# Sample tokens' retention attention cut into four pieces that stand between the weight matmuls of input units 23 and 24

## What is computed

```python
h = rmsnorm(x, g_pre_mix)
p = h @ w_in                     # 3328 columns: a_u a_v | b_b b_c b_x | c_q c_k c_v c_g
a_out = chunk_mlp(a_u, a_v)      # causal mixing in chunks of 128 tokens, 4 heads
b_out = b_b * conv3(b_c * b_x)   # depthwise, width 3, with a carried buffer
c_out = retention(rope(q), rope(k), v) normed per head * silu(c_g)     # 8 heads of 64
x = x + rmsnorm(concat(a_out, b_out, c_out) @ w_out)
x = x + rmsnorm((silu(h2 @ w_gate) * (h2 @ w_up)) @ w_down)            # h2 = rmsnorm(x)
```

```python
o = (q @ k.T * decay_mask) @ v + (q * q_decay) @ S      # S: that sequence's own 64 x 64 state
S = decay * S + (k * k_decay).T @ v
```

## Time and profile before

| | |
|---|---|
| three runs | 1314.28, 1316.05, 1316.15 us; median 1316.05 |
| the profiled execution | 1315.72 us |
| its span, first to last instruction | 1314.0 us |
| mean granted TensorE clock | 0.986 of full speed |
| PE busy | 1283.9 us (98% of the span) |
| DVE busy | 871.9 us (66%) |
| ACT busy | 558.3 us (42%) |
| DMA | 119.1 MB, mean 91 GB/s |

### The profile page before, as it was taken

How to read it: one execution, slowest core, us unless ns; L and a number is a source line. 1 busy time by engine, 2 the same in 40 slices (tenths; PEclk the granted TensorE clock), 3 DMA queues, 4 the chain that set the end, 5 groups by cost and what they waited for, 6 DMA issues and landing times.

```text
span 1314.0 us, 26201 instructions
## 1 busy us (share of the span) xinstructions
PE 1283.9 (98%) x10425; PEld 1253.8 (95%) x10425; DVE 871.9 (66%) x1231; ACT 558.3 (42%) x899; POOL 36.3 (3%) x60
## 2 busy tenths in 40 slices
PE   6999999989999999999999999998999999999997
PEld 6999998989999999999999999898999999999996
DVE  6855778288888787522586566855978787882225
ACT  4632224354355556522443512245444555562222
POOL 3000002000000000000020000010000000000000
PEclk9999998989999999999999999899999999999998
DMA  6322122123333333223242221132223333312321
GB/s 230 97 76 81 56 64 97 53 67 112 112 97 96 96 96 96 73 89 113 80 154 67 84 77 56 63 103 75 75 88 112 98 110 96 96 56 89 113 65 69
DMA packets 110410, 119.10 MB, mean 91 GB/s; under 512 B 4512, under 2 KB 107064, under 8 KB 110072
## 3 DMA queue, kind: packets, MB, share of 16 engines
q1 hardware_dynamic: 107392, 108.57, 26.2%
q0 software_dynamic: 2496, 8.24, 1.8%
q10 hardware_dynamic: 440, 1.09, 0.2%
HBM read 113.20 MB, written 4.69 MB: 90 GB/s over the span
## 4 chain that ended last, share of the span: by engine, by line
PE 90%; DVE 6%; ACT 1%; issue 1%; DMA 1%; ACTq 0%; DVEq 0%; SPq 0%
PE ps L608 20%; PE ps L610 19%; PE ps L609 19%; PE ps L990 8%; PE ps L992 8%; PE ps L991 8%; PE ps L638 1%; PE ps L758 1%; DVE w_lo L1384 1%; PE ps L777 1%; DVE x L1420 1%; PE ps L798 1%; DVE h_lo L1441 1%; DVE r_pre L1457 1%; PE ps L838 1%
## 5 line engine op out<-in xcount | busy, mean ns | idle before, releaser
L608 PE MATMUL ps<-h_hi,w_hi 128*128 128x272 f32 x1216 | 363.7, 299 | 8.9 <-issue 3.7
L610 PE MATMUL ps<-h_lo,w_hi 128*128 128x272 f32 x1216 | 354.1, 291 | 0.0
L609 PE MATMUL ps<-h_hi,w_lo 128*128 128x272 f32 x1216 | 352.7, 290 | 0.0
L1384 DVE TENSOR_TENSOR w_lo<-w_raw,w_hi 128x1024 fp32r<-128x1024 f32 (+1 forms) x140 | 165.1, 1190 | 176.5 <-ACT w_hi L1053 175.9
L990 PE MATMUL ps<-a_hi,p_hi 128*128 128x272 f32 x896 | 260.0, 290 | 2.3 <-DVE evac L1842 2.0
L992 PE MATMUL ps<-a_lo,p_hi 128*128 128x272 f32 x896 | 259.3, 289 | 0.0
L991 PE MATMUL ps<-a_hi,p_lo 128*128 128x272 f32 x896 | 257.9, 288 | 0.0
L608 PEld LDWEIGHTS ps<-h_hi,w_hi 128*128 128x128 f32 x1216 | 232.7, 191 | 17.9 <-issue 10.8
L609 PEld LDWEIGHTS ps<-h_hi,w_lo 128*128 128x128 f32 x1216 | 233.7, 192 | 2.3 <-issue 2.0
L610 PEld LDWEIGHTS ps<-h_lo,w_hi 128*128 128x128 f32 x1216 | 232.0, 191 | 0.0
L1053 ACT ACTIVATE w_hi<-w_raw 128x1024 fp32r<-128x1024 f32 (+1 forms) x140 | 143.2, 1031 | 168.1 <-DMA w_raw<-in_w_down 116.2
(11 more groups left out here) (203 smaller groups left out, 1654.9 us busy)
## 6 DMA issues: line engine op xcount, KB each, us to landing
w_raw<-in_w_in SPq DMA_DIRECT2D x52, 512.0 KB, 3.6
w_raw<-in_w_gate SPq DMA_DIRECT2D x44, 512.0 KB, 3.5
w_raw<-in_w_up SPq DMA_DIRECT2D x44, 512.0 KB, 3.5
w_raw<-in_w_down SPq DMA_DIRECT2D x40, 512.0 KB, 3.3
w_raw<-in_w_out SPq DMA_DIRECT2D x16, 512.0 KB, 3.4
tab<-in_table POOLq DMA_DIRECT2D x2, 1520.0 KB, 6.3
st_s<-in_state_ret POOLq DMA_DIRECT2D x8, 256.0 KB, 4.1
out<-st_s POOLq DMA_DIRECT2D x16, 128.0 KB, 2.2
```

What stands on the lines that cost most here:

```text
L608: pe.matmul(out, wh, hi[:, cols(half)], start=begins, stop=False)
L609: pe.matmul(out, wl, hi[:, cols(half)], start=False, stop=False)
L610: mm = pe.matmul(out, wh, lo[:, cols(half)], start=False, stop=ends)
L1384: vec.tensor_tensor(w_lo[s][:, 0:nk, :], w_raw[s][:, 0:nk, :], w_hi[s][:, 0:nk, :], ALU.subtract)\
```

## The change

`attend_s` is no longer one step behind unit 23. It becomes four pieces: the values matmuls with the state matmuls of head pair 0 stand in the middle of unit 23's second half; the state matmuls of head pair 1 directly behind unit 23, ahead of `norm_o3`; those of head pair 2 in the middle of unit 24's first half; those of head pair 3 and the two transposes in the middle of its second half. The middle of a half is behind two of its four k-tiles, 12 of 24 weight matmuls. The step now counts up `mix_pe` inside unit 24, behind `norm_o3`. Nothing is changed on DVE, ACT, POOL or SP but the counts they wait for.

```diff
-    23: ["attend_s", "norm_o3"], 24: ["norm_o4", "state_s0"], 25: ["state_s1"],
+    23: ["norm_o3"], "within 24": ["attend_s"], 24: ["norm_o4", "state_s0"], 25: ["state_s1"],
...
-            def unit(layer, pos, more, ks, source, group, first, last, done=None, before_half=lambda half: None):
+            def unit(layer, pos, more, ks, source, group, first, last, done=None, before_half=lambda half: None,
+                     mid_half=lambda half: None):
                 for half in range(2):
                     before_half(half)
-                    unit_half(layer, pos, more, ks, source, group, half, first, last, done)
+                    unit_half(layer, pos, more, ks, source, group, half, first, last, done,
+                              after_two=lambda half=half: mid_half(half))
...
-                def attend_s():
+                def attend_s_values():
                     after(probs_made, 5)
                     after(o_made, 4)
...
-                    for hp in range(HP):
-                        for b in range(DB):
...
+                def attend_s_state(hp):
+                    for b in range(DB):
+                        at = NS * hp + DS * b
+                        for e in range(2):
+                            rows = slice(HD * e, HD * e + HD)
+                            pe.matmul(ps[rows, 6, at:at + DS], st_s[rows, hp, b, :], qds[rows, hp, b, :],
+                                      start=False, stop=(b == DB - 1), skip_group_check=True)
+
+                def attend_s_end():
                     after(z_last_made, 1)
                     after(probs_made, 5)
                     for ct in range(2):
                         tr = transpose(ps[0:2 + 2 * DB, 5, P * ct:P * ct + P], z_last[:, ct, :], ident)
                     task_done(tr)
+                    assert task[0] == TASK["attend_s"]
+
+                def attend_s_between(u, half):
+                    if (u, half) == (23, 1):
+                        attend_s_values()
+                        attend_s_state(0)
+                    if u == 24:
+                        attend_s_state(2 + half)
+                        if half:
+                            attend_s_end()
...
                         unit(l, u, 0, range(4 * kh, 4 * kh + 4), from_h, 0, kh == 0, kh == 1,
-                             win_done if kh else None, before)
+                             win_done if kh else None, before, lambda half, u=u: attend_s_between(u, half))
+                    if u == 23:
+                        attend_s_state(1)
                     for name in TASKS_AFTER.get(u, []):
                         tasks[name]()
```

More of the change, by code:

```diff
@@ L885, in _ @@
                          "turn_av": turn_av, "turn_av_s": turn_av_s, "mix_tokens": mix_tokens,
-                         "mix_tokens_s": mix_tokens_s, "attend_s": attend_s,
+                         "mix_tokens_s": mix_tokens_s,
                          "state_s0": lambda: state_s(0, (4, 5)), "state_s1": lambda: state_s(1, (6, 7))}
```

## The result

| | before | changed |
|---|---|---|
| five runs, us | 1314.28 to 1316.15, median 1315.85 | 1320.69 to 1324.83, median 1323.69 |
| ratio of the times, 95% interval | | 1.0061 (1.005 to 1.0073) |
| profiled execution | 1315.72 | 1320.81 |
| its span | 1314.0 | 1319.0 |
| mean granted clock | 0.986 | 0.989 |

The change makes the kernel 6.6 to 9.6 us slower. The traced pair differs by 5.1 us, nearly the 5.4 forecast; the medians differ by 7.8, and the changed kernel's median stands 0.1 us above the range.

The account below looks back on a forecast made before the run. PE, busy 98% of the span, was taken as the bound, with layer 1's chain on DVE ahead of unit 24. +0.35 us plus 2 x 2.5 for the clock made +5.4 on 1315.72: 1321.1 us, range 1317.8 to 1323.6.

Parts of the forecast that it names:

- What bounds: Around units 23 to 25, layer 1's chain of waits runs over DVE from 828.95; `attend_s` fills a gap DVE leaves anyway.
- Parts (1) and (2): Values and head pair 0 inside unit 23 cost nothing; ahead of unit 24, PE's wait grows from 0.65 to about 2.5 us.
- Part (3): Head pairs 2 and 3 and the transposes add 2.54 us to unit 24, making 8.59 us at full clock.
- The rival in which PE hides the pieces: Unit 24's pieces overlap the weight matmuls around them; clock held, 4.7 us faster, 1311.0 us; chance 0.05.
- Part (5): Between units 23 and 24 the clock falls in both layers, costing unit 24 2.0 to 3.1 us per layer, middle 2.5.
- the rule that was weighed against the rows: The skill blames idle gaps between matmul bursts; by it the 2.5 us gap is too short, leaving the sum at +0.35.
- Part (6): Consumers behind unit 24: ACT's and DVE's later work, 11.3 us, hides under PE's 11.8 us before `w_out`, 0.5 us to spare.
- The sum: +0.35 us plus 2 x 2.5 for the clock, +5.4 us on the profiled 1315.72: 1321.1 us.
- part (4): Clock held, `norm_o4` starts at 211.3 (+0.4) in layer 0 and 850.15 (-0.05) in layer 1: together +0.35 us.
- I leave it there: The forecast of 1321.1 us was left unadjusted, the profiled execution standing 0.3 us below the runs' median of 1316.05.

Follow-up runs that it names:

- e1: Changed kernel with head pairs 1 to 3 and the transposes together behind unit 23, before `norm_o3`, none inside unit 24: 1314.6 us, 1.0001 of before.
- e3: Changed kernel with two DVE steps, `expand(0)` and `a_lo_g`, moved behind the eviction of `G01`: 1311.6 us, 0.9979 of before.
- e8: Changed kernel with PE's order as in e1 and DVE's order as in e3, a repeated run: 1313.06 us, 0.9992 of before.
- e2: Changed kernel with 20 extra weight matmuls that nobody reads behind `norm_o3`, where PE waits for DVE: 1316.53 us, 1.002 of before.
- e5: Changed kernel without the state matmuls of head pairs 2 and 3, transposes still inside unit 24: 1316.06 us, 1.0007 of before.

## Why the prediction was right in its mechanism and wrong in its size

*What bounds (the chain on DVE, `attend_s` free in the gap)*: right, shown by e1 and e3. Undoing the move of two pairs and the transposes takes the loss away, and shortening DVE's chain turns the change into a gain.

*Parts (1) and (2), PE's wait grows to about 2.5 us*: right, 2.53 us in both layers and in all three traces.

*Part (3), 2.54 us inside unit 24*: right, 8.70 us measured with the clock held against 8.59. The rival in which PE hides the pieces is out.

*Part (5), the clock falls in both layers*: right, in six of six layer passes. Here the rule that was weighed against the rows goes under. The Trainium skill ("TensorE: Matmul & The Clock Gate", section "Why this matters for your kernels") would have the clock keep through an idle gap as short as this; it fell behind 2.53 us of idle time, and in e8 behind none. Where the page goes by idle time alone, the measurement decides.

*Part (6), consumers*: right, and with little to spare. Measured back from the first unit of `w_out`, ACT's `ab_hi` starts 4.5 to 7.4 us later than before and the two halves of DVE's eviction of `G23` 1.4 and 0.7 us later; the second half ends 0.36 us ahead of that unit (1.03 us before), where the prediction had 0.5 us. That unit follows `norm_o4` by 10.27 us in every trace of both kernels, so none of it reached PE.

*The sum*: this is the step that failed. Two of its terms are the clock's price, and I took each from one execution, with 6.8 us for every fall. First, the credit in part (4): the old marks at 210.89 and 850.20 hold 6.8 us of low clock in each layer, and the sum lets the pieces' 5.1 us be paid almost in full by that. But the old kernel's low stretch is 3.4 us in the second trace, and the stages are 1.48 and 1.69 us shorter there: the credit was up to 3.2 us too large. On the chip of e2 the term that was forecast as +0.35 us measured +2.8 (1316.53 - 1313.76, interval 1.4 to 3.7 us). Second, part (5)'s bounds of 2.0 to 3.1 us per layer: unit 24 took 1.3 to 3.8 us more than 8.70 in the three traces. The mean of the six, 2.4 us, is the forecast's 2.5; the ends are not. A low stretch of 10.2 us was nowhere in the old trace; but one of 3.4 us was, near the start of the kernel, and the prediction made no use of it:

```profile
17.80:21.20 3.40, 2.97 (x13) 3.00 (x14) 3.40 (x7) 3.40 (x7) 3.40 (x8) 0.50 0.91 314
```

What makes a stretch long stays open. The changed kernel's traces would fit the idea that a small piece that runs in the low stretch prolongs it: the 6.8 us of layer 1 above and the 10.2 us hold one, the 3.4 us stretches end as one begins, and without pairs 2 and 3 none was over 6.8 us. But stretches of 6.8 us also come without a state piece (unit 24 of the old kernel's layer 1, e5's above), and it was not tested apart from the time that the pairs take.

So "I leave it there", the sentence that puts the profiled execution next to the median and is done, was the mistake: the medians compare executions with different low stretches, and mine were one of each. Both layers' stages together take 67.7 to 68.4 us in the three traces of the changed kernel, and 62.8 and 59.6 in the two of the old one. The difference is 5.0 to 8.8 us: the forecast of 5.4 stands near its lower end, and the range, which ended 7.9 us above the profiled execution, should have reached its upper end.

That the traced pair came within 0.3 us of the forecast is partly luck. The base was no outlier among its own five runs (1315.72 against a median of 1315.85), but the changed kernel's traced execution is 2.9 us below the median of its five. Its stages have 3.4 and 6.8 us of low clock and not 10.2, and of all thirteen traces of these experiments it is the only one in which the low clock at the entry to layer 0's feed-forward part lasts 3.4 us and not the 6.8 of the earlier trace rows:

```profile
280.46:283.87 3.41, 3.00 (x13) 3.03 (x14) 3.38 (x4) 1.46 (x3) 0.00 (x0) 0.50 0.02 5
```

What stays open: the changed kernel's second and third trace are 2.2 to 2.6 us longer than the first, but only 0.7 us of it lies in the stages. Most of the rest is between the stages, with the entry to the feed-forward part (1.2 us), and ahead of unit 23 (0.4 and 0.6 us), where both kernels have the same code and the low clock also lasts 3.4 or 6.8 us from one execution to the next. Whether the change shifts the odds there was not tried, so how the 2.4 us between the forecast and the difference of the medians divide between the stages and these places is not measured.

## What to carry to other kernels

Before work is moved off a stretch that looks bad, ask which engine ends that stretch: work that stands where its engine would wait anyway is free, and moved between that engine's other instructions it is paid in full (8.70 us for unit 24 with the clock held, against the 6.05 worked out without pieces). Here the spreading itself was sound, and became a gain (0.9979, 0.997 to 0.9989) as soon as the eviction that PE waited for was put ahead of two DVE steps that nobody was waiting for. And a price that the clock sets differs between executions of one program: take it from several traces of both sides before a range is made.

## What the runs showed that I had not expected

20 matmuls whose result nobody reads make the changed kernel 6.9 us faster. And the low clock comes in stretches of 3.4, 6.8 and 10.2 us in one and the same program; the old kernel's 29 executions on one chip, 1311.9 to 1318.4 us, have mean clocks from 0.989 to 0.983, the lower ones by and large in the longer executions.
